# Feed-forward on the transposed sum, its root factored out behind the first product, with work moved at both ends of each feed-forward

## The reference

```
def rmsnorm(x, g):
    y = x * rsqrt(mean(x * x, axis=-1) + EPS)
    return y * g

def conv_glu_ffn(h, w_in, conv_w, conv_b, w_out):   # h = rmsnorm(x, ffn_norm_g)
    u = h @ w_in                                    # (256, 2 * 2752)
    up = pad(u, two tokens of zeros in front)
    c = conv_b + sum(up[:, tap:tap + S] * conv_w[tap] for tap in range(3))
    return (silu(gate half of c) * value half of c) @ w_out
```

## Time and profile before

| | us |
|---|---|
| median of 3 runs | 673.42 (672.68 to 677.87) |
| the profiled execution, its own time | 673.4 |
| its span, first to last instruction | 671.6 |

### The profile page before, as it was taken

The page is one execution under the profiler, slowest core; times in us unless marked ns, Lnnn a source line. Parts: engine busy times, 40 slices in busy tenths (PEclk is TensorE's granted clock), DMA queues, the critical chain, the costliest instruction groups (busy, mean ns, idle before and its releaser), DMA issues.

```text
span 671.6 us, 11001 instructions
## 1 busy us (share of the span) xinstructions
PE 641.3 (95%) x3662; PEld 537.4 (80%) x3662; DVE 511.6 (76%) x990; ACT 415.9 (62%) x856; POOL 20.8 (3%) x69
## 2 busy tenths in 40 slices
PE   8999989989999999999998999979899999999994
PEld 7988766678888888888887788757788888888893
DVE  4587578965888888888877556796788888888886
ACT  6554367836766666666657445673966666666655
POOL 2100000000000000000002000051000000000000
PEclk9999989999999999999999999999999999999998
DMA  7675020037255555555542545305355555555521
GB/s 274 236 272 205 15 120 2 2 125 251 98 193 191 196 200 196 200 196 198 197 142 75 187 178 188 126 2 196 150 189 189 190 194 187 197 201 196 202 73 64
DMA packets 21442, 109.02 MB, mean 162 GB/s; under 512 B 2592, under 2 KB 2976, under 8 KB 12448
## 3 DMA queue, kind: packets, MB, share of 16 engines
q1 hardware_dynamic: 21120, 108.36, 45.0%
q10 hardware_dynamic: 288, 0.22, 0.1%
HBM read 107.52 MB, written 1.05 MB: 162 GB/s over the span
## 4 chain that ended last, share of the span: by engine, by line
PE 78%; DVE 10%; ACT 5%; issue 3%; POOL 2%; DMA 1%; POOLq 0%; SPq 0%; ACTq 0%; DVEq 0%
PE psA L397 12%; PE psA L398 12%; PE psA L399 12%; PE psO L500 10%; PE psT L500 10%; PE psO L505 5%; PE psT L505 5%; DVE win_lo L1338 2%; DMA stage<-in_w_group 1%; ACT arena L1161 1%; DVE stat L1607 1%; PE psT L676 1%; PE psA L659 1%; DVE x L1388 1%; PE psO L691 1%
## 5 line engine op out<-in xcount | busy, mean ns | idle before, releaser
L1440 DVE TENSOR_TENSOR win_lo<-stage,win_hi 128x1024 fp32r<-128x1024 f32 x90 | 109.6, 1219 | 5.6 <-ACT win_hi L1012 5.6
L1457 DVE SCALAR_TENSOR_TENSOR arena<-arena,prm 128x255 f32<-128x255 f32 (+1 forms) x152 | 73.5, 484 | 50.7 <-ACT arena L1038 48.0
L1012 ACT ACTIVATE win_hi<-stage 128x1024 fp32r<-128x1024 f32 x92 | 96.1, 1051 | 10.0 <-PE psA L399 5.6
L500 PE MATMUL psO<-hA,win_hi 128*128 128x512 f32 x304 | 95.5, 395 | 0.0
L500 PE MATMUL psT<-hA,win_hi 128*128 128x512 f32 x304 | 95.1, 394 | 0.0
L1338 DVE TENSOR_TENSOR win_lo<-stage,win_hi 128x1024 fp32r<-128x1024 f32 (+3 forms) x58 | 64.6, 1154 | 24.8 <-ACT win_hi L948 24.5
L1038 ACT ACTIVATE arena<-arena,prm 128x256 f32<-128x256 f32 x76 | 45.7, 602 | 58.4 <-DVE arena L1463 58.1
L948 ACT ACTIVATE win_hi<-stage 128x1024 fp32r<-128x1024 f32 (+3 forms) x56 | 53.5, 1002 | 28.4 <-PE psA L399 19.2
L397 PE MATMUL psA<-wout_hi,act_hi 128*128 128x512 f32 x176 | 69.2, 393 | 0.7 <-DVE act_lo L1506 0.5
L398 PE MATMUL psA<-wout_lo,act_hi 128*128 128x512 f32 x176 | 68.7, 390 | 0.0
L399 PE MATMUL psA<-wout_hi,act_lo 128*128 128x512 f32 x176 | 68.5, 389 | 0.0
(11 more groups left out here) (287 smaller groups left out, 1218.6 us busy)
## 6 DMA issues: line engine op xcount, KB each, us to landing
stage<-in_w_ffn_in SPq DMA_DIRECT2D x44, 1024.0 KB, 5.5
stage_out<-in_w_ffn_out SPq DMA_DIRECT2D x44, 516.0 KB, 3.6
stage<-in_w_kv SPq DMA_DIRECT2D x8, 1024.0 KB, 4.8
stage<-in_w_group SPq DMA_DIRECT2D x5, 1024.0 KB, 5.0
stage<-in_w_nsa_out SPq DMA_DIRECT2D x4, 1024.0 KB, 5.6
stage<-in_w_dq SPq DMA_DIRECT2D x4, 1024.0 KB, 4.8
stage<-in_w_dout SPq DMA_DIRECT2D x4, 1024.0 KB, 4.8
stage<-in_w_phi SPq DMA_DIRECT2D x2, 1024.0 KB, 4.9
```

Of the source, the lines that this page charges most:

```text
L500: mm(o, win_hi[:, slot, cs], hA[:, k, :, :].rearrange("p a q -> p (a q)"), start=k == 0, stop=False)
L1012: act.activation(win_hi[:, slot, h * W // 2:(h + 1) * W // 2], stage[:, slot, h * W // 2:(h + 1) * W // 2], ACT.Copy).then_inc(sem["in_hi" ...
L1440: last = dve.tensor_tensor(win_lo[:, slot, cs], stage[:, slot, cs], win_hi[:, slot, cs].bitcast(F32), sub)
L1457: dve.scalar_tensor_tensor(conv[:, b, g, k:S], src[:, 0:S - k], prm[:, b, 4 * g + 2 - k:4 * g + 3 - k], conv[:, b, g, k:S], ALU.mult, ALU. ...
```

## The change

What it does, part by part:

- The feed-forward no longer waits for the norm. PE transposes x itself (`raw_T`): the first token half inside the last chunk of the out projection, the second in `up_raw`, which is the product of chunk 0, done by 128-row steps k in the order 0, 2, 1, 3, 4, 6, 5, 7 (`T_ORDER`), each as soon as its hi and lo are written, into psA. `stay_warm`, `xsT` and the writing of xs go.
- The inverse roots are computed meanwhile on DVE (`newton_a` to `newton_d`, for both token halves at once), spread to 128x256 (`rows_of_rstd`), transposed by PE (`row_T`) and copied by ACT to `row`: every partition holds the 256 tokens' roots.
- u is multiplied by `row` on DVE: for chunk 0 and chunk 20 straight from PSUM (`times_row`), for the others by a second operation after the add (`add_and_scale`), for chunk 21 into u_part. The two 256-wide adds become one of 512, and so do ACT's two copies of the lo sums.
- A step's order changes: DVE splits the first half of chunk j+2 between the scaling and the taps, and ACT before the start of the convolution.
- The last two chunks are interleaved (`last_steps`); lo of product 20 comes after the taps of chunk 21, and in layer 0 half a K/V chunk is split in between.
- In the NSA attention three of the four parts of out-projection chunk 0 run inside turns 13, 14 and 15; DVE splits chunk 0 in turns 10 and 11 and chunk 1 in turns 14 and 15.
- In the first projections DVE splits the next chunk before the rotary step instead of after it; behind the first feed-forward the second half of hB is written after one more split.

The diff, cut. PE:

```diff
-            def stay_warm(n, out, w, h):
...
-            def xsT(n):
...
-                for t in range(TT):
-                    pe_.wait_ge(sem["scaled_dve"], TT * (n - 1) + t + 1)
-                    xT_part(xs, t, range(KT // 2))
-                    pe_.wait_ge(sem["scaled_act"], TT * (n - 1) + t + 1)
-                    xT_part(xs, t, range(KT // 2, KT))
-                    if t == 0:
-                        stay_warm(4, psA[:, 0, 0:S], hB_hi[:, 0, 0:P], hB_hi[:, 0, :])
...
+            def raw_T(n, t, half):
+                pe_.wait_ge(sem["x_new"], 2 * TT * X_NEW[n] + 2 * t + half + 1)
+                xT_part(x, t, range(half * KT // 2, (half + 1) * KT // 2))
...
+                for k in ks:
+                    kk = 2 * c + k
+                    for n in range(2):
+                        if kk == KT - 1 and t == TT - 1:
+                            raw_T(n_norm, 0, n)
+                        cs = slice(k * D + n * 512, k * D + n * 512 + 512)
+                        last = three(psA[:, 2 * t + n, :], h_hi[:, kk, t * P:(t + 1) * P], h_lo[:, kk, t * P:(t + 1) * P],
+                                     win_hi[:, slot, cs], win_lo[:, slot, cs], kk == 0, kk == KT - 1)
+                        if kk == KT - 1 and t + n < 2:
+                            last.then_inc(sem["y_ready"], 1)
+                if t == TT - 1 and ks[-1] == 1:
+                    last.then_inc(sem["in_used"], 1)
...
+                if u >= len(UNITS) - 3:
+                    i = u - (len(UNITS) - 3)
+                    pe_.wait_ge(sem["negmax"], len(UNITS) - 1 + i // 2)
+                    pe_.wait_ge(sem["probs"], 4 * (len(UNITS) - 1 + i // 2))
+                    out_part(C_WO, hB_hi, hB_lo, 0, 2 * TT, 0, i // 2, (i % 2,), 1)
...
+            out_part(C_WO, hB_hi, hB_lo, 0, 2 * TT, 0, 1, (1,), 1)
+            out_project(C_WO, hB_hi, hB_lo, 0, 2 * TT, 1, chunks=range(1, 4))
...
+                def up_raw(h_waits, n):
+                    raw_T(n, 1, 0)
+                    slot = first % 2
+                    pe_.wait_ge(sem["in_hi"], 2 * (first + 1))
+                    pe_.wait_ge(sem["in_lo"], first + 1)
+                    for i, k in enumerate(T_ORDER):
+                        if i == 2:
+                            raw_T(n, 1, 1)
+                        pe_.wait_ge(sem["xT_hi"], h_waits + i + 1)
+                        pe_.wait_ge(sem["xT_lo"], h_waits + i + 1)
+                        for g in range(2):
+                            cs = slice(k * 2 * P + g * P, k * 2 * P + g * P + P)
+                            last = three_w(psA[:, g, 0:S], slot, cs, k, i == 0, i == KT - 1)
...
+                def row_T():
+                    pe_.wait_ge(sem["row_src"], layer + 1)
+                    for t in range(TT):
+                        last = pe_.transpose(psA[:, 2, t * P:(t + 1) * P], row_src[:, t, :], ident[:, :])
+                    last.then_inc(sem["row_bank"], 1)
...
+                def up_second():
...
+                        pe_.wait_ge(sem["in_hi"], 2 * (first + 1) + kh + 1)
+                        if kh == 0:
+                            pe_.wait_ge(sem["half_lo"], layer + 1)
+                        else:
+                            pe_.wait_ge(sem["in_lo"], first + 2)
+                        for g in range(2):
+                            last = up_pairs(g, 1, slot, range(kh * KT // 2, (kh + 1) * KT // 2))
+                    last.then_inc(sem["in_used"], 1)
```

ACT:

```diff
-                    act.wait_ge(sem["u_bank"], j + (f0 + 1))
+                def conv_first(j, b, g, src):
+                    act.activation(conv[:, b, g, :], src, ACT.Identity,
...
+                def step(j, b, halves=True):
...
+                    act.wait_ge(sem["in_used"], j + (first + 1))
+                    if halves:
+                        act.activation(u_part, psU[:, b, :, S:2 * S], ACT.Copy).then_inc(sem["u_part"], 1)
+                    split_in(j + 2, b, 0)
+                    act.wait_ge(sem["u_norm"], j + (f0 + 1))
...
+                        conv_first(j, b, g, u_sum[:, g, :])
...
-                    if split_next:
-                        split_in(j + 2, b, 1)
+                    split_in(j + 2, b, 1)
                     act.wait_ge(sem["prod"], j + (f0 + 1))
...
+                def last_steps():
...
+                    if layer == 0:
+                        split_in(NJ, 0, 0)
...
+                    act.wait_ge(sem["prod"], j + (f0 + 1))
+                    act.wait_ge(sem["out_used"], j + (f0 - 1))
+                    act.activation(act_hi[:, 0, :], prod[:, 0, :], ACT.Copy).then_inc(sem["a_hi"], 1)
...
-                normalise()
-                h_hi(hA_hi, O_FG + layer * KT, 1 if layer == 0 else 3)
+                inst, waits = (1, KT) if layer == 0 else (3, 4 * KT)
+                if layer == 0:
+                    act.wait_ge(sem["eps_ready"], 1)
+                act.activation(warm, eps, ACT.Sqrt)
+                square_halves(n, 0)
+                root_of(n, 0)
+                raw_hi(layer, inst, waits, 0)
+                raw_hi(layer, inst, waits, 2)
+                square_halves(n, 1)
+                raw_hi(layer, inst, waits, 4)
+                root_of(n, 1)
+                raw_hi(layer, inst, waits, 6)
                 split_in(1, 1, 0)
+                act.wait_ge(sem["row_bank"], layer + 1)
+                act.activation(row, psA[:, 2, 0:S], ACT.Copy).then_inc(sem["row_ready"], 1)
                 split_in(1, 1, 1)
```

DVE:

```diff
+                def add_and_scale(j, b):
+                    add_parts(j, b)
...
+                    dve.wait_ge(sem["u_sum"], j + layer * (NJ - 3))
+                    dve.tensor_tensor(u_sum, u_sum, rows, ALU.mult).then_inc(sem["u_norm"], 1)
...
+                def step(j, b):
+                    add_and_scale(j, b)
+                    split_in(j + 2, b, 0)
+                    taps(j, b)
+                    product(j, b)
+                    split_in(j + 2, b, 1)
+                    product_lo(j, b)
+                    split_out(j + 1, 1 - b)
...
+                    dve.wait_ge(sem["rstd_t"], TT * ROOTS[n] + TT)
+                    dve.tensor_copy(row_src, rstd.unsqueeze(2).to_broadcast([P, TT, P])).then_inc(sem["row_src"], 1)
...
+                    j = NJ - 2
+                    times_row(j, psU[:, 0, :, 0:S])
+                    take_params(j + 1, 1)
+                    taps(j, 0)
+                    product(j, 0)
+                    if layer == 0:
+                        split_in(NJ, 0, 0)
...
+                    dve.wait_ge(sem["in_used"], first + NJ)
+                    dve.tensor_tensor(u_part[:, 0, :], psT[:, 1, 0:S], row, ALU.mult).then_inc(sem["u_norm"], 1)
...
-                        dve.scalar_tensor_tensor(conv[:, 1, 0, k:S], psT[:, 1, 0:S - k], taps[2 - k], conv[:, 1, 0, k:S],
+                        dve.scalar_tensor_tensor(conv[:, 1, 0, k:S], u_part[:, 0, 0:S - k], prm[:, 1, 2 - k:3 - k], conv[:, 1, 0, k:S],
                                                  ALU.mult, ALU.add).then_inc(sem[done], 1)
+                    product_lo(j, 0)
...
-                normalise(lambda h: split_in(0, 0, h))
-                h_lo(hA_lo, hA_hi, O_FG + layer * KT)
...
+                split_in(0, 0, 0)
+                add_y(n, 0, 0, "in_used", first)
+                add_y(n, 0, 1, "in_used", first)
+                split_in(0, 0, 1)
+                add_y(n, 1, 0, "in_used", first)
+                first_mean(n, 0)
+                add_y(n, 1, 1, "in_used", first)
+                raw_lo(0)
+                raw_lo(1)
+                raw_lo(2)
+                raw_lo(3)
+                first_mean(n, 1)
                 take_params(0, 0)
+                split_out(0, 0)
+                raw_lo(4)
+                newton_a()
+                raw_lo(5)
+                newton_b()
+                raw_lo(6)
+                newton_c()
+                raw_lo(7)
+                newton_d()
+                rows_of_rstd()
                 split_in(1, 1, 0)
+                dve.wait_ge(sem["row_ready"], layer + 1)
+                times_row(0, psA[:, 0:2, 0:S])
                 split_in(1, 1, 1)
-                split_out(0, 0)
-                step(0, 0, halves=False)
+                take_params(1, 1)
+                taps(0, 0)
+                product(0, 0)
+                split_in(2, 0, 0)
+                product_lo(0, 0)
+                split_in(2, 0, 1)
+                split_out(1, 1)
...
-                step(NJ - 2, 0, layer == 0, False, halves=False)
-                last_step()
+                last_steps()
...
-                        rope(tokA[:, :, h0:h0 + nh, :], tokB[:, :, h0:h0 + nh, :], nh)
...
                 if c + 2 < N_A:
                     split(c + 2)
+                if c % 2 and kind == "q":
+                    rope(tokA[:, :, h0:h0 + nh, :], tokB[:, :, h0:h0 + nh, :], nh)
+                if c % 2 and kind == "k":
+                    rope(k_tok, k_tok, 8)
...
-                if u >= NU - 2:
```

(4 more changed lines are left out.)

269 lines of the change are left out of this document (129 added, 140 removed).

## The result

Against 22 runs of the kernel before beside it (median 674.28 us), the changed kernel's 22 runs have a median of 677.24: ratio 1.0038, interval [1.0021, 1.0054]. Forecast were 672.8 and a range of 668.5 to 675.5. Its profiled execution took 674.18 with a span of 672.4, so it is one of its quicker runs. Its profile shows none of the signs that the forecast named for being wrong: the granted clock is 1.00 from 174 to 190, the gap before down(0) is 2.54, and the loop's period is 8.29 (8.42 once, from down(1) to down(2)) with PE busy all the time.

A forecast was written before the change was run, and what follows sets the result against it. TensorE, busy 641.3 of 671.6 us, was taken to bound the kernel. From 673.4, terms of -0.65, -0.9, -0.65, 0, +1.0, +0.6 and 0 summed to -0.6: 672.8 us, with an 8-in-10 range of 668.5 to 675.5.

The forecast's parts named there:

- signs that the forecast named for being wrong: Loop period above 8.3, granted clock below 1.00 at 175 to 190, or gap before down(0) under 1 us.
- Step 1: First projections: TensorE's waits of 0.39 and 0.26 for VectorE's lo halves go, with the split first; -0.65 us.
- Step 2: End of NSA attention: out-projection parts cover waits of 1.18 and 0.77, new gaps of about 1.1 open; -0.9 us.
- Step 3: Start of each feed-forward: first product 4.1 us earlier, but down(0) waits 2.6 for a_lo(0); -0.35 each, -0.65 both.
- Step 4: Feed-forward loop: VectorE gets about 0.55 us more per step, hidden by TensorE's period of 8.29; 0.
- rival (b): Loop becomes VectorE's when its chain exceeds 8.29; at 8.5 the loops lose 7 us, giving 680; chance 0.05.
- Step 5: End of each feed-forward: a_lo(20) comes later and delays down(20); +1.0 us in layer 0, +0.6 in layer 1.
- Step 6: K/V projections behind layer 0: second half of hB comes one split later, within slack; 0, up to +0.2 us.
- (c): Clock falls at a feed-forward's start without stay_warm's matmuls, costing 2 to 2.5 us per layer: 677.5; chance 0.06.
- (a): Feed-forward's start gives its full 3.3 us per layer, -6.6 instead of -0.65: 667 us; chance 0.1.

The follow-up runs named there:

- both fillers: Changed kernel plus unread matmuls (fillers), 18 ahead of down(0) in each layer and 14 ahead of down(20) in layer 0: 675.0 us, ratio 1.0024.

## Why the forecast was wrong, step by step

- **Step 1** (-0.65): the waits of 0.39 and 0.26 are gone, one of 0.21 is new; the attention starts 1.1 us earlier, 0.3 of which is an earlier first product, not of this step, so 0.8. Right.
- **Step 2** (-0.9): new waits 0.39 + 0.76 against 1.95 gone. The out projection's end, without the transposes now inside it, gains 0.4 behind turn 12 rather than 0.9: mis-sized by half a us. Steps 1 and 2 together, undone, cost 1.4 by the means and 2.9 by the ratios.
- **Step 3** (-0.35 each): the first product starts 1.56 behind the end of the out projection instead of 6.54, and with the 0.9 of transposes that moved ahead of that end this is the 4.1 of the forecast. Down(0) waits 2.54 (2.6), and -0.5 is left at down(1), in either layer. (The sum has -0.65 for both layers where twice -0.35 is -0.7.) ScalarE's next instruction starts 0.02 behind the load, so the drain that the Trainium skill gives in "ScalarE: Activation LUTs", section "What ACT_TABLE_LOAD costs", shows no more in this trace than in the earlier trace rows:

```profile
171.08 0.39 ACT L1137 ACTIVATE arena<-psA 128x256 f32<-128x256 f32 x1 [1.46 <-PE psA L504]
171.36 1.05 ACT L1047 ACTIVATE win_hi<-stage 128x1024 fp32r<-128x1024 f32 x1
172.43 1.28 ACT L1140 ACT_TABLE_LOAD   x1
173.73 0.20 ACT L1140 ACTIVATE stat<-stat 128x1 f32<-128x1 f32 x1
```

- **Step 4** (0): PE is busy for 155.93 of 156, DVE +0.53 per step against +0.55. Right; rival (b) did not come.
- **Step 5** (+1.0, +0.6): down(19) starts at 340.49, 2.6 before the old 343.05, and the K/V transposes that wait for the new x at 353.49, 0.1 behind the old 353.38. Of these 2.7 us 1.6 are clock and 1.1 order. In layer 1, from down(19) to the last matmul, the order costs 1.0 with a wait of 0.75 ahead of down(20), 0.4 more than forecast. The order was right in layer 0 and mis-sized in layer 1; that this very wait of 1.96 is one where the clock can fall was not thought of.
- **Step 6** (0): from those transposes to the last units of the differential attention the changed kernel takes 91.85 instead of 92.20, so 0.35 less. No cost, as forecast.
- **What failed** is that steps 3 and 5 price the waits that they open, 2.6 ahead of each down(0) and nearly 2 ahead of down(20), by their length alone: the clock's fall behind them stands in the sum with nothing and in the rivals as (c), "the clock falls at a feed-forward's start", with 0.06. The reason was the earlier trace rows, where the clock was still 1.00 some 3 us into TensorE's last idle time; from it I took it that a wait of 2.6 is harmless. But a fall comes at the wait's end or up to 2 us behind it, as the rows at 180 to 186 show, so that the work pays for it, while nothing followed that last idle time. The two waits ahead of down(0) are places where the clock falls in 6 of 10 cases at 1.4 us each, and the one ahead of down(20) or down(21) in 3 of 8, at 1.6 in the changed kernel. Together that is some 2.3 us of the 3.2 that the clock costs (2.8 between the means, and the 0.4 that the order gives in the pair of traces). Where the rest is lost is open; the attentions' falls differ from run to run in both kernels.
- **That (c)'s 677.5 stands next to the measured 677.2 is luck.** It priced a fall in each layer's start at 2 to 2.5 us; measured are 1.3 to 1.4, and in 6 of 10 cases, and a share of the loss comes from the end of layer 0, which (c) did not name. Its 4 to 5 us at the lower level had no row.
- **The range** does not follow from the terms named for it: half of (a)'s gain ends at 670.1 and not at 668.5, and with the upper bounds of steps 2 and 5 (+1.8 for each layer) the sum is 676.1, not 675.5. The measured 677.2 lies outside either.

The Trainium skill says in "TensorE: Matmul & The Clock Gate", section "Part 4: PE-mode transpose", that transposes don't count as busy like matmuls do. No run here tests it, and the dearest falls do not start behind transposes. Those of 88 to 98 come while PE is busy for 2.00 of 2.00 us, and all fifteen start during or just behind 32 matmuls of only 32 columns, ahead of the next transposes. First the changed kernel, with no fall, then the one with both fillers:

```profile
88.40 3.71 PE L735 MATMUL psU<-rope_t,qT 128*128 128x32 f32 x32
...
89.12 5.04 PE L741 MATMUL psU<-rope_t,qT 128*128 128x32 f32 x32
```

Whether these narrow matmuls draw the fall is not shown.

What stays open: whether falls avoided at one place come at another (the fillers' gains did not add), and why the feed-forward's waits of 1.96 to 2.54 us are followed by falls and those up to 1.55 are not; no feed-forward here has a wait between.
